# RWKV head sums from hi and lo fp32r pieces in a one-core hybrid encoder layer

## The reference

```python
kk = split_h(k * p['rwkv_k_k'])
kk = kk / jnp.maximum(jnp.sqrt(jnp.sum(kk * kk, axis=-1, keepdims=True)), 1e-12)
...
s_state, y = lax.scan(rwkv_step, f32(s_state), ...)
y = time_major(y)
mu = jnp.mean(y, axis=-1, keepdims=True)
var = jnp.mean(jnp.square(y - mu), axis=-1, keepdims=True)
y = (y - mu) * lax.rsqrt(var + RWKV_GN_EPS) * gn_g + gn_b
bonus = jnp.sum(r * k * r_k, axis=-1, keepdims=True) * v
out = (y + bonus).reshape(bsz, t, RWKV_W) * jax.nn.silu(z)
```

## Time and profile before

| what | value |
|---|---|
| median of 3 runs | 2261.97 us (2260.13 to 2261.99) |
| the profiled execution's own time | 2262.04 us |
| its span, first to last instruction | 2260.2 us |
| mean granted TensorE clock | 0.998 |
| TensorE matmuls busy | 2227.2 us, 99% of the span |
| TensorE weight loads busy | 2165.2 us, 96% |
| VectorE busy | 1321.6 us, 58% |
| ScalarE busy | 779.5 us, 34% |

### The profile page before, as it was taken

One profiled execution on the slowest core, in us unless ns is written; L12 is line 12 of the kernel. 1 busy time (PEld: TensorE's weight loads), 2 busy tenths in 40 slices (PEclk: granted clock), 3 DMA queues, 4 the chain that ended last, 5 costly groups with the idle time before them and its releaser, 6 DMA issues.

```text
span 2260.2 us, 44650 instructions
## 1 busy us (share of the span) xinstructions
PE 2227.2 (99%) x18965; PEld 2165.2 (96%) x18965; DVE 1321.6 (58%) x2052; ACT 779.5 (34%) x1180; POOL 56.5 (2%) x83
## 2 busy tenths in 40 slices
PE   6999999999999999999999999999999999999998
PEld 5999999999999999999999998989999999999997
DVE  5434433488777777767465554646657664454354
ACT  5321222234333333334242433333333352334343
POOL 0000001000000000000000000000000000000000
PEclk9999999999999999999999999999999999999999
DMA  5422222133343324343021212113221344344465
GB/s 181 139 71 95 78 89 88 65 113 111 121 139 105 135 105 144 96 148 125 21 94 39 74 59 75 57 44 135 89 71 60 105 169 171 137 157 169 141 213 185
DMA packets 67064, 249.33 MB, mean 110 GB/s; under 512 B 9051, under 2 KB 16397, under 8 KB 50069
## 3 DMA queue, kind: packets, MB, share of 16 engines
q1 hardware_dynamic: 66916, 247.14, 31.5%
HBM read 216.92 MB, written 30.19 MB: 109 GB/s over the span
## 4 chain that ended last, share of the span: by engine, by line
PE 98%; DMA 1%; DVE 0%; SPq 0%; ACT 0%; issue 0%; DVEq 0%; POOL 0%; ACTq 0%; POOLq 0%
PE acc L997 53%; PE acc L1187 15%; PE branch L1187 7%; PE acc L1577 7%; PE branch L1577 2%; PE branch L1277 1%; PE branch L1483 1%; PE branch L1302 1%; PE branch L1293 1%; PE acc L1040 1%; DMA scratch<-in_x_all 1%; PE branch L1132 1%; PE branch L1125 0%; PE branch L1267 0%; PE branch L1345 0%; PE branch L1597 0%
## 5 line engine op out<-in xcount | busy, mean ns | idle before, releaser
L997 PE MATMUL acc<-act_hi,w_hi 128*128 128x320 f32 (+2 forms) x2912 | 888.2, 305 | 0.0
L997 PE MATMUL acc<-act_lo,w_hi 128*128 128x320 f32 (+2 forms) x2912 | 863.2, 296 | 0.0
L997 PE MATMUL acc<-act_hi,w_lo 128*128 128x320 f32 (+2 forms) x2912 | 863.1, 296 | 0.0
L997 PEld LDWEIGHTS acc<-act_hi,w_hi 128*128 128x128 f32 x2912 | 548.1, 188 | 14.0 <-issue 5.0
L997 PEld LDWEIGHTS acc<-act_lo,w_hi 128*128 128x128 f32 x2912 | 548.3, 188 | 0.7
L997 PEld LDWEIGHTS acc<-act_hi,w_lo 128*128 128x128 f32 x2912 | 548.2, 188 | 0.0
L2104 DVE TENSOR_TENSOR w_lo<-w_raw,w_hi 128x2048 fp32r<-128x2048 f32 x121 | 277.1, 2290 | 247.7 <-ACT w_hi L1635 245.3
L1635 ACT ACTIVATE w_hi<-w_raw 128x2048 fp32r<-128x2048 f32 x122 | 233.6, 1914 | 134.1 <-PE branch L1577 119.9
L1187 PE MATMUL acc<-corner_terms,w_hi 128*128 128x288 f32 x736 | 148.1, 295 | 0.0
L1187 PE MATMUL acc<-act_hi,w_hi 128*128 128x288 f32 x496 | 146.6, 296 | 0.0
L1187 PE MATMUL acc<-act_lo,w_hi 128*128 128x288 f32 x496 | 146.4, 295 | 0.0
(11 more groups left out here) (461 smaller groups left out, 3437.3 us busy)
## 6 DMA issues: line engine op xcount, KB each, us to landing
w_raw<-in_w_stream SPq DMA_DIRECT2D x124, 1024.0 KB, 4.8
w_raw<-in_w_stream SPq DMA_DIRECT2D x92, 512.0 KB, 5.5
gate_logits<-gate_out SPq DMA_DIRECT2D x48, 288.0 KB, 2.4
scratch<-gate_logits SPq DMA_DIRECT2D x48, 288.0 KB, 5.3
scratch<-in_x_all SPq DMA_DIRECT2D x9, 512.0 KB, 6.1
branch_rows<-branch_out SPq DMA_DIRECT2D x16, 288.0 KB, 2.2
scratch<-in_x_all SPq DMA_DIRECT2D x3, 1024.0 KB, 10.7
out_y_prompt<-scratch SPq DMA_DIRECT2D x6, 512.0 KB, 2.9
```

The costliest lines, as they stand in the source:

```text
L997: last = mm(acc[s][:, at:at + hi - lo], a[:, s, w], b[:, k, lo:hi], start=(k == order[0] and a is whi and b is xh), stop=(k == order[-1] a ...
```

## The change

The lengths, the means and the variances no longer run in plain fp32. ScalarE writes the moving rows once more, rounded to fp32r (hi), VectorE subtracts that from the rows (lo), and TensorE runs both pieces, for each half of the columns, against an fp32r copy of `blocks`, made once ahead of the loop. The bonus stays as it is. That is one ScalarE pass and one VectorE pass over 128 x 592 more for each of the three sums, and four fp32r matmuls in place of two fp32 ones. The means move from block 58 to 60, the turn of the states from 61 to 62, the variances from 61 to 64, which is behind the last block of N(5). The lengths stay at block 9. VectorE's `y_rows_lo` is put ahead of `split_lo(N(6))`, and `kk_squares_lo` behind the reciprocal of step `a`.

```diff
     "rwkv_vector":
-        ... k_step k kk_raw a kk_floor
+        ... k_step k kk_raw a kk_squares_lo kk_floor
...
-        y_centred y_unit y_affine y_bonus y""",
+        y_rows_lo y_centred y_squares_lo y_unit y_affine y_bonus y""",
...
+        blocks_r = sb("head_blocks", P, F32R)
...
+        sum_hi, sum_lo = ([tsum[:, a + T * h:a + T * h + T] for a in (x3, x1_sums + 1280)] for h in range(2))
...
+                def head_sums(bank, m, step):
+
+                    for h in range(2):
+                        tok = slice(HALF * h, HALF * h + HALF)
+                        mm(bank[:, 512 * h:512 * h + HALF], blocks_r[:, :], sum_hi[m][:, tok], start=True, stop=False)
+                        last = mm(bank[:, 512 * h:512 * h + HALF], blocks_r[:, :], sum_lo[m][:, tok], start=False, stop=True)
+                    pt.done(last, step)
+
                 def lengths():
-                    pe.wait_ge(*at.after(i, "kk_squares"))
-                    for h in range(2):
-                        last = mm(bra[:, 512 * h:512 * h + HALF], blocks, ctmp[:, HALF * h:HALF * h + HALF], start=True, stop=True)
-                    pt.done(last, "kk_lengths")
+                    pe.wait_ge(blocks_here, 1)
+                    pe.wait_ge(*vt.after(i, "kk_squares_lo"))
+                    head_sums(bra, 0, "kk_lengths")
...
                 def means():
-                    pe.wait_ge(*vt.after(i, "state5"))
-                    pe.wait_ge(*at.after(i, "out4"))
...
+                    pe.wait_ge(*vt.after(i, "y_rows_lo"))
+                    head_sums(bra, 1, "y_sums")

                 def variances():
-                    pe.wait_ge(*at.after(i, "y_squares"))
...
+                    pe.wait_ge(*vt.after(i, "y_squares_lo"))
+                    head_sums(brb, 1, "y_square_sums")
...
-                plan += [(block, means), (block + 3, turn_states), (block + 3, variances)]
+                plan += [(block + 2, means), (block + 4, turn_states), (block + 6, variances)]
...
             act.wait_ge(states_out, 16 * (2 * NH_A + 2))
+            act.wait_ge(consts_here, 16)
+            f(blocks_r[:, :], blocks, ACT.Copy).then_inc(blocks_here, 1)
             with looped(act, 0, NP_C) as i:
...
                 S.done(f(ctmp, kk, ACT.Square), "kk_squares")
+                S.done(f(sum_hi[0], kk, ACT.Square), "kk_squares_hi")
...
+                    elif c == NCH - 1:
+                        act.wait_ge(*S.after(i, "out4"))
+                        S.done(f(sum_hi[1], ysb, ACT.Copy), "y_rows_hi")
                 act.wait_ge(*V.after(i, "y_centred"))
                 S.done(f(ysq, yc, ACT.Square), "y_squares")
+                S.done(f(sum_hi[1], yc, ACT.Square), "y_squares_hi")
...
                 V.done(v.reciprocal(ca, ca), "a")
+                dve.wait_ge(*S.after(i, "kk_squares_hi"))
+                tt(sum_lo[0], ctmp, sum_hi[0].bitcast(F32), ALU.subtract, "kk_squares_lo")
                 dve.wait_ge(*G.after(i, "kk_lengths"))
...
+                dve.wait_ge(*S.after(i, "y_rows_hi"))
+                tt(sum_lo[1], ysb, sum_hi[1].bitcast(F32), ALU.subtract, "y_rows_lo")
                 split_lo(N(6))
                 dve.wait_ge(*G.after(i, "y_sums"))
                 V.done(v.scalar_tensor_tensor(out=split2(yc), in0=halves(bra), scalar=-1.0 / 64, in1=split2(ysb), op0=ALU.mult, op1=ALU.add), "y_centred")
-                own("state5")
+                dve.wait_ge(*S.after(i, "y_squares_hi"))
+                tt(sum_lo[1], ysq, sum_hi[1].bitcast(F32), ALU.subtract, "y_squares_lo")
                 dve.wait_ge(*S.after(i, "y_rstd"))
```

More of the change, by code:

```diff
@@ L291 @@
     "rwkv_vector": """
-        vectors negated streams_apart ranks1 decay log_decay log_sums log_decay_sums k_step k kk_raw a kk_floor
+        vectors negated streams_apart ranks1 decay log_decay log_sums log_decay_sums k_step k kk_raw a kk_squares_lo kk_floor
         k_factor k_new kk kkh b bE kE bh kh r_step r end_decays rh bonus_terms bu0 bu1 uk0 uk1 yb0 yb1 low0
@@ L295 @@
         w1 bonus state0 z1 z2_part low6 z2 inv6 gate tv u0 state1 u1 state2 u2 state3 u3 state4 u4 state5
-        y_centred y_unit y_affine y_bonus y""",
+        y_rows_lo y_centred y_squares_lo y_unit y_affine y_bonus y""",
     "rwkv_scalar": """
-        rank_exps decay_exps kk_squares kk_log kk_rsqrt kk_rows bE_rows kE_rows t0 v_rows
-        t1 t2 t3 t4 z_exp t5 tk out0 out1 out2 out3 out4
-        y_squares y_log y_rstd state_out""",
+        rank_exps decay_exps kk_squares kk_squares_hi kk_log kk_rsqrt kk_rows bE_rows kE_rows t0 v_rows
+        t1 t2 t3 t4 z_exp t5 tk out0 out1 out2 out3 out4 y_rows_hi
+        y_squares y_squares_hi y_log y_rstd state_out""",
     "rwkv_tensor": """
@@ L679, in build @@
         x_used = sem("x_blocks_used")
+        blocks_here = sem("head_blocks_rounded")
         y_hi, y_split, z_hi, z_split = sem("branch_hi_done"), sem("branch_split"), sem("merged_hi_done"), sem("merged_split")
@@ L1417, in means @@
                 def means():
-                    pe.wait_ge(*vt.after(i, "state5"))
-                    pe.wait_ge(*at.after(i, "out4"))
-                    for h in range(2):
-                        last = mm(bra[:, 512 * h:512 * h + HALF], blocks, ysb[:, HALF * h:HALF * h + HALF], start=True, stop=True)
-                    pt.done(last, "y_sums")
+                    pe.wait_ge(*vt.after(i, "y_rows_lo"))
+                    head_sums(bra, 1, "y_sums")
                 def variances():
-                    pe.wait_ge(*at.after(i, "y_squares"))
-                    for h in range(2):
-                        last = mm(brb[:, 512 * h:512 * h + HALF], blocks, ysq[:, HALF * h:HALF * h + HALF], start=True, stop=True)
-                    pt.done(last, "y_square_sums")
+                    pe.wait_ge(*vt.after(i, "y_squares_lo"))
+                    head_sums(brb, 1, "y_square_sums")
                 def turn_states():
```

## The result

The changed kernel takes 2283.3 us (median of four runs, 2281.94 to 2284.7) against 2261.37 of the kernel before beside it: a ratio of 1.0097, 95% interval 1.0083 to 1.0111. It is 22 us slower; 2280 was forecast, range 2270 to 2287.

The account below looks back on a forecast made before the run. TensorE was taken to bound the kernel, any wait it gets adding in full. Head 0's lengths 1.5, heads 1 to 3 at 4.9 each, last head's end 0.3 and clock 1.5 made 18.0 over 2262.0: 2280 us, range 2270 to 2287.

Parts of the forecast that it names:

- The sums: Twelve sums of four fp32r matmuls, 0.55 us each instead of 1.0; net 5.0 us saved if nothing waits.
- The end of a head: TensorE waits 0.7 us at the turn of the states, 0.4 at the variances; a head's end becomes 0.3 us longer.
- The lag handed on: ScalarE's Ln after a head's end, and the VectorE and ScalarE chain behind it, come 2.7 us later.
- The lengths behind the reciprocal: At block 9 TensorE waits for `kk_squares_lo`: 2.0 us in head 0 (+1.5), 5.0 in heads 1 to 3 (+4.9 each).
- Next in line: Behind the lengths, at `kk_turned`: the meeting of VectorE and TensorE gets looser and no further wait follows.
- The clock: Slow TensorE matmuls behind the new mid-kernel waits of 5.0 us: 1.5 us taken, between ends of nothing and 6.4.
- the rival that had 0.18: TensorE's clock falls in all three long gaps: 16.5 + 6.4, giving 2285 us; chance 0.18.

Follow-up runs that it names:

- fitted kernels: Three kernels with pieces for the lengths, the means, or both, queues refitted and variances in plain fp32, against the kernel before: 2260.79, 2260.28 and 2258.79 us.

## Why the prediction was right, point by point

- **The sums** (0.55 instead of 1.0 us): right. At the means of head 0 the first tile matmul starts 0.55 us after the sum's first (1148.28 to 1148.83); behind a wait it is 0.64, at head 0's lengths. The fitted kernels keep 0.3 to 0.4 us a sum where nothing waits, somewhat less than 0.45. It was 5 us against waits four times as large.
- **The end of a head**: mechanism right, sizes somewhat high. Waits of 0.7 and 0.4 us were forecast at the turn and at the variances; from start to start they are 0.54 (1150.96 - 1150.29 - 0.13) and 0.37 (1153.09 - 1152.59 - 0.13). The next head's first tile began 0.1 us later than before against head 0's lengths, not 0.3. The second ScalarE pass starts 0.1 us ahead of the first one's end, which the sum did not use.
- **The lag handed on**: right, 2.5 us instead of 2.7, and shown alone by the run with plain lengths.
- **The lengths behind the reciprocal**: right, +1.5 us in head 0, and waits of 5.0 us from start to start (4.83 in the list) in each of heads 1 to 3, as the sum had it; a head costs 4.7 where 4.9 stood; the run with plain means and variances shows the reciprocal's own part.
- **Next in line**: the sum said that nothing waits behind the lengths, and nothing did. But the text named `kk_turned` as next, and in the run with late lengths the weights of N(2) came first.
- **The clock**: the one term that was mis-sized. It was put at 1.5 us, on the ground that gaps of 5 us in dense work are a smaller thing than the start's 13.8; it is 6.3, in all three gaps. What happened is the rival that had 0.18 (the clock falls in all three long gaps, 2285), and the measured 2283.3 is nearer to it than to 2280. That the time lies in the range is owed to the upper bound, which was set by this rival. That its 6.4 meets 6.3 so well is partly luck: it was three times 2.1 from one stretch at the start, and the three were 2.7, 2.0 and 1.6. The rule of the Trainium skill (TensorE: Matmul & The Clock Gate, Part 1: The HAM clock gate), that idleness halves the clock until activity brings it back, is what the trace shows here behind the three long gaps: a granted clock of 0.50, then 1.00 again. The gap of 1.7 us in head 0 left it at 1.00.

The balance of the profiled spans: 2282.9 - 2260.2 = 22.7 us. Slow matmuls are 6.3. TensorE's start is 0.6 later, ahead of any changed matmul, and is taken as chance: the waits at the start add up to 20.9 to 21.9 us over the ten profiles. The waits leave 15.8 after the savings, where 16.5 were forecast. The forecast sum was 18.0, so 4.7 too few in the profiled run: the clock's 4.8 and the start's 0.6, less 0.7 too many for the waits. By the medians 2280 was 3.3 us low.

## What to carry to other kernels

Where TensorE is the bound, as here, an operand that is cheaper for it but needs two more passes on other engines can cost more in waits than it saves. Look for what already stands in the queue at the place where the new pass is put (here a 3.85 us reciprocal and a 2.28 us split), and for the slack of the step that waits for it. A lag at the end of one iteration comes back in the next, and here two short waits that met in one place made a gap in which the clock fell too. In this kernel the remedy was in the order of the queues: a long operation cut in two, a pass done chunk by chunk, and a stage one block later.

## What the runs showed of the hardware that was not expected

- The clock fell at each of the six gaps of 4.8 us (three in the changed kernel, three with the split first) and at none of the three gaps of 2.4 us (means and variances plain). But at the gaps of 2.25 us of the run with late lengths it fell in three heads of four, some 1 us after the matmuls had begun again and ahead of the second wait. So gap length alone does not tell; what else decides stays open.
- The fall came 2.3 to 4.9 us after the matmuls had stopped, in the six long gaps and the three short ones, whether or not they had begun again.
- How long the matmuls then stayed slow differed from 3.5 to 6.0 us behind equal gaps in the changed kernel. The stretches at 1.2 GHz themselves last 3.4 us (three) or 6.8 us (six); what lies in the gap costs nothing.
- A page whose clock row reads full speed throughout hid 6.3 us of slow matmuls; the mean clock of the run, 0.995 against 0.998, was the only hint ahead of the narrow slices.
